# A norm applied behind the products of four projection units instead of ahead of them, and gate projections two blocks ahead in a grouped attention

## The chip, the cores and the metric

One core of a Trainium2 chip runs the whole program. The metric is the device time of one execution in microseconds (us). Four compute engines work side by side and meet at semaphores: PE (TensorE, matrix products into the eight banks of PSUM), DVE (VectorE), ACT (ScalarE) and POOL (GpSimd, which here never touches PSUM). SP starts most of the loads. Each engine runs its own list of instructions strictly in order.

## The reference, cut to what matters

The input (512 tokens of 1024 features, and 256 context tokens) goes through a first block (norm, two grouped attentions, gated up-projection, MLP) and then through two blocks with adaptive norms. The change touches two places. In the first block two gates are computed from the same normed input as the attention:

```python
y = jax.nn.sigmoid(gate_a) * (o_a @ w_up_nsa[l]) + jax.nn.sigmoid(gate_b) * (o_b @ w_up_swa[l])
...
f = jnp.square(jax.nn.relu(u @ w_mlp_in[l])) @ w_mlp_out[l]
h = h + rms_norm(f, norm_mlp_post[l])
```

and right behind that MLP the second block normalises the result and projects it to queries, keys, values and gates of eight heads:

```python
hx = modulate(rms_norm_2(x, norm_g[i]), shift_x[:, None], scale_x[:, None])   # h * (1 + scale) + shift
hc = modulate(rms_norm_2(ctx, norm_g[i]), shift_c, scale_c)
...
qx, kx, vx, gx = split(hx @ w_in)
qc, kc, vc, gc = split(hc @ w_in)
```

The norm's factor, one over the root mean square, is one number for each token; gain, scale and shift are one number for each feature. So hx @ w is that factor times ((x * gain * (1 + scale)) @ w), plus shift @ w.

## The kernel before, in words

Everything lies transposed, features on the 128 partitions and tokens along the row; a tensor of 1024 features is eight tiles k = 0 to 7 of 512 token columns (and 256 context columns). Weights come in **units** of 1024 x 128. Each unit is loaded by SP, rounded to fp32r on ACT (`split_high`, L330), and the rest of it is taken on POOL (`low`, L973). A product is then three matmuls for each k: high by high, low by high, high by low (`products`, L347 and L351). The units have one order through the whole program, and the slots of their two halves alternate between two places (`SPL`), with a few exceptions in the table `THIRD`. A unit's `split_high` waits until the unit before last is done on PE.

**The first grouped attention** (`A1`). After the phase "prep" all engines meet. PE does the scores of steps 0 and 1, then `attn_pe` walks 62 blocks of 128 keys: each block is a transposition of four heads' weights (L570), then a gate tile (`gate_tiles`, two k of a gate unit, six matmuls into bank 5), then the weighted sum of the block before (L581); scores of later steps (L551) stand between. DVE takes minima (L675) and scales (L710), ACT does the exponentials (L636) and moves the transposed block (L621). Every fourth block ACT moves a finished gate unit out (`gate_out`, L867), rounds the next unit, POOL multiplies the gate by the norm, and ACT later takes the tanh and stores it by DMA. The 16 gate units are 64 such tiles; the last two stand behind the last block, and then PE waits until the last output group is split on ACT (L745) and DVE (L750, semaphore `A1.ol`) and begins the up-projections.

**From the MLP to the first head.** The last MLP round ends with eight accumulations into `f_t`. PE sums their squares over the features (`column_sums`, L415, matmuls of one column each), ACT takes the root, DVE inverts, and `spread` (L430) brings the factor to all partitions in bank 5. DVE then scales and adds, tile by tile (L2087, L2093), giving `hc`; ACT squares each tile (L1578), PE sums each (`tile_sum`). In between PE does the context products of the first two units of the heads' projection, whose context input was made during the MLP. With the second root (L1580), DVE's reciprocal and a second `spread` into bank 7, the normed input is made: `x_tile` on DVE (L1988), `shift_tile` on ACT (L1527), `low_tile` on DVE (L1994), for k = 0 to 7, and units 0 and 1 follow them staggered; units 2 and 3 (value and gate) come whole through `project`. ACT evicts each (L1596 to L1602). DVE rotates queries and keys (`rotate`, L2123 to L2132, six operations each), and `gate_up` (L2138) makes the gate.

**The heads.** `attend` on PE does for each of eight heads the scores of six query tiles (L1311), transpositions of the weights (L1323) and the two weighted sums (L1347, L1355), and between them `dense(n)`, n of the 32 k-steps of the next head's four units (`project`). A k-step is six matmuls, three of 512 and three of 256 columns. On DVE `mins` (L2184) and `combine` (L2192 to L2199) work on each query tile, then the next head's two rotations; on ACT the exponentials (L1640), and `take` moves each finished unit out of the banks. `take` of the next head's key unit stands inside the fifth query tile's exponentials.

## Time and profile before

| what | value |
|---|---|
| median of 3 runs | 1629.29 us (1629.1 to 1634.57) |
| the profiled execution's own time | 1629.36 us |
| its span in the profile | 1627.2 us |
| mean granted clock of TensorE | 0.984 of full |
| PE busy | 1556.7 us, 96% |
| DVE, ACT, POOL busy | 985.8, 751.7, 504.6 us |
| share of PE in the chain that ended last | 80% |

The profile page gives busy times and, for the chain, which engine's work the end waited for at each step. The two places of the change lie at 130 to 335 us (the first attention) and at 788 to 899 us (from the last MLP product to the second head) of the span. The granted clock is given as a share of full speed: 1.00 is 2.4 GHz and 0.50 is 1.2 GHz.

### The profile page before, as it was taken

What the parts mean: (1) busy time and instruction counts of PE and PEld (TensorE: products, weight loads), DVE (VectorE), ACT (ScalarE), POOL (GpSimd) and SP (SyncE); (2) the same over time, 40 slices, a digit from 0 to 9 for tenths busy, and PEclk for the clock granted to TensorE, in tenths of its full rate; (3) what the DMA queues carried; (4) which work ended last, traced back from release to release, by engine and by line L of the source; (5) the groups of instructions that cost most, each with busy time, mean ns of one, the idle gap of its engine ahead of it and who ended that gap; (6) DMA issues with size and microseconds to landing.
All of it is one profiled execution on the core that took longest, in us unless ns stands there. A gap on an engine that the chain in (4) does not pass through costs nothing.

```text
span 1627.2 us, 23677 instructions
## 1 busy us (share of the span) xinstructions
PE 1556.7 (96%) x8392; PEld 1221.3 (75%) x8392; DVE 985.8 (61%) x2266; ACT 751.7 (46%) x1413; POOL 504.6 (31%) x231
## 2 busy tenths in 40 slices
PE   7998999999899999999899999999999989999997
PEld 5886666678688888888877877778777768876566
DVE  6235555355679867645666666675676267147854
ACT  6225766634342423234344554455445343248753
POOL 3651232245244444444221111121214354230012
PEclk9999999999999999999899999999999989999999
DMA  6861112264356565643111111111111122220001
GB/s 200 174 162 33 59 59 77 76 256 130 104 193 194 191 198 188 198 134 100 53 53 39 40 39 39 39 39 39 39 39 52 52 56 89 78 66 14 2 14 65
DMA packets 48401, 149.34 MB, mean 92 GB/s; under 512 B 5782, under 2 KB 9110, under 8 KB 48184
## 3 DMA queue, kind: packets, MB, share of 16 engines
q1 hardware_dynamic: 37080, 112.45, 23.0%
q10 hardware_dynamic: 11232, 35.72, 6.8%
q8 instruction: 54, 0.88, 0.2%
q14 instruction: 35, 0.29, 0.1%
HBM read 141.53 MB, written 6.62 MB: 91 GB/s over the span
## 4 chain that ended last, share of the span: by engine, by line
PE 80%; DVE 7%; ACT 5%; issue 5%; POOL 1%; DMA 1%; ACTq 0%; POOLq 0%; DVEq 0%; SPq 0%
PE ps L347 41%; PE ps L351 20%; PE ps L570 4%; PE ps L581 3%; PE ps L551 3%; PE ps L1347 3%; PE ps L1311 2%; PE ps L1323 1%; POOL w_l L973 1%; PE ps L415 1%; PE ps L1075 1%; ACT sb L636 1%; DVE tg L1921 1%; ACT w_h L330 1%; DVE b_sb L675 1%
## 5 line engine op out<-in xcount | busy, mean ns | idle before, releaser
L973 POOL TENSOR_TENSOR w_l<-raw,w_h 128x1024 fp32r<-128x1024 f32 (+1 forms) x190 | 457.0, 2406 | 897.1 <-ACT w_h L330 877.4
L330 ACT ACTIVATE w_h<-raw 128x1024 fp32r<-128x1024 f32 x190 | 200.7, 1058 | 360.5 <-PE ps L347 305.3
L347 PE MATMUL ps<-x2h,w_h 128*128 128x512 f32 (+1 forms) x816 | 245.3, 366 | 19.5 <-DVE x2l L1994 7.6
L347 PE MATMUL ps<-x1h,w_h 128*128 128x512 f32 x584 | 237.9, 407 | 16.0 <-POOL w_l L973 10.4
L347 PE MATMUL ps<-x2h,w_l 128*128 128x512 f32 (+1 forms) x816 | 231.8, 349 | 0.0
L351 PE MATMUL ps<-x2l,w_h 128*128 128x512 f32 (+1 forms) x816 | 231.7, 349 | 0.0
L347 PE MATMUL ps<-x1h,w_l 128*128 128x512 f32 x584 | 230.7, 395 | 0.0
L351 PE MATMUL ps<-x1l,w_h 128*128 128x512 f32 x584 | 230.1, 394 | 0.0
L347 PEld LDWEIGHTS ps<-x2h,w_h 128*128 128x128 f32 x816 | 132.4, 191 | 52.6 <-issue 17.1
L347 PEld LDWEIGHTS ps<-x2h,w_l 128*128 128x128 f32 x816 | 132.2, 191 | 20.8
L351 PEld LDWEIGHTS ps<-x2l,w_h 128*128 128x128 f32 x816 | 132.5, 191 | 19.5
L347 PEld LDWEIGHTS ps<-x1h,w_h 128*128 128x128 f32 x584 | 111.5, 191 | 40.5 <-POOL w_l L973 10.8
L347 PEld LDWEIGHTS ps<-x1h,w_l 128*128 128x128 f32 x584 | 111.1, 190 | 24.3
L351 PEld LDWEIGHTS ps<-x1l,w_h 128*128 128x128 f32 x584 | 111.7, 191 | 20.4
L2055 DVE CUSTOM_DVE_ANT_0 terms<-mraw,ps 128x1024 f32<-128x1024 f32 x96 | 116.8, 1216 | 2.5
L2184 DVE CUSTOM_DVE_ANT_0 a_p<-ps,small 128x768 f32<-128x768 f32 (+1 forms) x96 | 71.3, 776 | 58.4 <-issue 58.4
L347 PE MATMUL ps<-m_h,w_h 128*128 128x512 f32 x256 | 99.7, 389 | 0.0
L347 PE MATMUL ps<-m_h,w_l 128*128 128x512 f32 x256 | 99.6, 389 | 0.0
L351 PE MATMUL ps<-m_l,w_h 128*128 128x512 f32 x256 | 99.6, 389 | 0.0
L1640 ACT ACTIVATE a_p<-a_p,small 128x768 f32<-128x768 f32 (+1 forms) x96 | 75.2, 786 | 20.4 <-DVE small L2184 20.4
L980 POOL TENSOR_TENSOR g_stage<-g_stage,rstd 128x512 f32<-128x512 f32 x16 | 20.6, 1286 | 148.2 <-ACT g_stage L867 148.2
L636 ACT ACTIVATE sb<-sb,small 128x256 f32<-128x256 f32 (+4 forms) x128 | 59.7, 471 | 4.2 <-ACT g_stage L872 1.9
(318 smaller groups left out, 2615.3 us busy)
## 6 DMA issues: line engine op xcount, KB each, us to landing
raw<-in_w_mlp SPq DMA_DIRECT2D x64, 512.0 KB, 3.7
mraw<-in_w_mod ACTq DMA_DIRECT2D x51, 512.0 KB, 3.7
raw<-in_w_a SPq DMA_DIRECT2D x32, 512.0 KB, 3.6
raw<-in_w_att SPq DMA_DIRECT2D x25, 512.0 KB, 11.3
raw<-in_w_b SPq DMA_DIRECT2D x20, 512.0 KB, 3.6
raw<-in_w_g SPq DMA_DIRECT2D x16, 512.0 KB, 3.6
raw<-in_w_ao SPq DMA_DIRECT2D x9, 512.0 KB, 3.5
gates<-g_stage ACTq DMA_DIRECT2D x16, 256.0 KB, 2.2
```

The lines of the kernel that those rows point to most:

```text
L330: nc.scalar.activation(split(u)[0], raw[:, u % RAW], ACT.Copy).then_inc(w_hi, 1)
L347: mm = nc.tensor.matmul(o, w[:, k], xh(k), start=(first and k == k0 and wi == 0), stop=(last and k == k1 - 1 and wi == 1))
L351: mm = nc.tensor.matmul(o, w[:, k], xl(k), start=False, stop=False)
L551: mm = nc.tensor.matmul(A.sbank(m + h)[:, o:o + rhs.shape[-1]], st[qx](r + h), rhs, start=(x == 0), stop=(x == last), skip_group_check=True)
L570: mm = nc.tensor.transpose(ps[0:w, 4 + x % A.tb, y * P:(y + 1) * P], A.sb[n % A.sbn][:, r, o:o + w], ident[:])
L581: mm = nc.tensor.matmul(ps[h * HD:(h + 1) * HD, 6 + g % 2, cols], st["v"](h)[b], A.pt[0:w, x % 4, h * 2 * P:(h + 1) * 2 * P], start=(st["f ...
L636: nc.scalar.activation(buf, buf, ACT.Exp, bias=negm[:, c:c + 1], scale=-1.0, accum_out=sums[:, c:c + 1]).then_inc(A.e, 1)
L973: nc.gpsimd.tensor_tensor(l[:, ks], raw[:, u % RAW, ks], h[:, ks].bitcast(F32), ALU.subtract).then_inc(w_lo, 1)
L1347: mm = nc.tensor.matmul(ps[:, 6], a_v[:, b, :], a_pt[:, b, :], start=(b == 0), stop=(b == 5))
L1640: nc.scalar.activation(buf, buf, ACT.Exp, bias=negm[:, cc:cc + 1], scale=-1.0, accum_out=sums[:, cc:cc + 1]).then_inc(ha["e"], 1)
L2055: nc.vector.tensor_tensor_reduce(out=terms[:], in0=mraw[:, c % MRAW].rearrange("p k m -> p (k m)"), in1=cps[:, w, :], scale=0.5, scalar=0. ...
L2184: nc.vector.tensor_tensor_reduce(out=a_p[qt % 3][m][:, 0:n], in0=pair(1 + 2 * m)[:, 0:n], in1=zero.to_broadcast([P, n]), scale=1.0, scalar ...
```

## The change

The gate tiles run two blocks ahead: tiles 0 and 1 go between the scores of steps 0 and 1, block x does tile x + 2 and none is left behind the last block; ACT's `gate_out` is moved with them. Behind the MLP, the first four units of the heads' projection use an input without the norm's factor (`xph`, `xpl`), made tile by tile as `hc` is; the shift's part comes out of two more columns of the context product (258 instead of 256), and DVE multiplies each of the four results in PSUM by the factor, and ACT (or DVE, for the gate) adds the shift. The full input with the norm is made after that, for the other units. Nine of the 32 k-steps of head 1 stand ahead of head 0's first scores, and the gate of head 0 is finished between its two rotations. Unit 2 gets a place of its own (`w_h4`, `w_l4`).

```diff
-THIRD = {..., U_MLP + 2: 2}
+THIRD = {..., U_MLP + 2: 2, U_A + 2: 3}
+AHEAD = 2
...
-        A1.between_pe, A1.between_act = gate_tiles, gate_out
+        A1.between_pe, A1.between_act = lambda pe, x: gate_tiles(pe, x + AHEAD), lambda act, x: gate_out(act, x + AHEAD)
...
-            attn_scores(pe, A1, 0)
-            attn_scores(pe, A1, 1)
+            for x in range(AHEAD):
+                attn_scores(pe, A1, x)
+                gate_tiles(pe, x)
             attn_pe(pe, A1)
-            for x in range(A1.blk[-1], N_G * KT // 2):
+            for x in range(A1.blk[-1] + AHEAD, N_G * KT // 2):
                 gate_tiles(pe, x)
...
             nm3a.wait(pe, "add", KT - 1)
             column_sums(sqsum, 4, S, True, False)
+            pe.wait_ge(ml_f, 4 + N_MLP - 2)
+            first_ctx(0, 1, 0, 2)
             nm3a.wait(pe, "sq", KT)
             column_sums(sq[:, 1], 4, S, False, True).then_inc(nm3a.mm, 1)
+            first_ctx(0, 1, 2, 4)
             nm3a.wait(pe, "rc", 1)
             nm3c.wait(pe, "lo", KT)
             spread(5, 0, 4).then_inc(nm3a.r, 1)
+            first_ctx(0, 1, 4, KT)
             pe.wait_ge(ml_f, 4 + N_MLP)
-            first_ctx(0, 0, KT)
-            tile_sum(0)
-            first_ctx(1, 0, KT // 2)
-            tile_sum(1)
-            first_ctx(1, KT // 2, KT)
-            for k in range(2, KT):
+            first_ctx(1, 3, 0, KT)
+            for k in range(KT):
                 tile_sum(k)
+                nm3p.wait(pe, "lo", k + 1)
+                for j in range(2):
+                    mm = first_x(j, 2 * j, k, k + 1)
+                    if k == KT - 1:
+                        mm.then_inc(unit, 1)
+            first_x(2, 4, 0, 4)
             nm3b.wait(pe, "rc", 1)
             spread(7, 0, 4).then_inc(nm3b.r, 1)
-            for k in range(KT + LAG):
-                if k < KT:
-                    nm3b.wait(pe, "lo", k + 1)
-                    mm = first_x(0, k)
-                    ...
-                if k >= LAG:
-                    mm = first_x(1, k - LAG)
-            mm.then_inc(unit, 1)
+            first_x(2, 4, 4, KT)
+            nm3b.wait(pe, "src", KT)
+            first_ctx(2, 5, 0, KT).then_inc(unit, 1)
+            first_ctx(3, 6, 0, KT)
+            wait_head(pe, "k", (None, 0), 1, 1)
+            first_x(3, 2, 0, KT).then_inc(unit, 1)
...
+                lead = i is None and c == 0
+                if lead:
+                    dense(9)
+                    wait_head(pe, "g", head, 1, 1)
                 wait_head(pe, "ro", head, 2, 2)
                 scores(0)
-                dense(2 if more else 3)
+                dense(1 if lead else 2 if more else 3)
...
                 scores(1)
-                dense(4 if more else 3)
+                dense(2 if lead else 4 if more else 3)
                 for qt in range(4):
                     scores(qt + 2)
-                    dense(2 if more else 4 + (qt == 0))
+                    dense(1 if lead else 2 if more else 4 + (qt == 0))
                     turns(qt)
-                    dense(1 + qt % 2 if more else 3)
+                    dense(1 + qt // 2 if lead else 1 + qt % 2 if more else 3)
                 turns(4)
-                dense(4)
+                dense(2 if lead else 4)
...
-            project((None, 0), 2 * KT, 2 * KT)
             pe.wait_ge(ha["ones"], 1)
             all_heads(pe, attend)
```

On ACT:

```diff
             mlp(3, False, True)
+            split_high(act, U_A + 2)
...
             for k in range(KT):
                 nm3b.wait(act, "src", k + 1)
+                nc.scalar.activation(xph[:, k, :], hc[:, k, 0:S], ACT.Copy, scale=mulx[:, 0, 0, k:k + 1]).then_inc(nm3p.hi, 1)
...
+            nm3b.wait(act, "r", 1)
+            nc.scalar.activation(rstd[:, 0:S], ps[:, 7], ACT.Copy).then_inc(n3_r, 1)
+            split_high(act, U_A + 3)
+            def take_first(j, dst, scale):
+                wait_head(act, "em", (None, 0), 8, 2 * j + 2)
+                nc.scalar.activation(dst[:, S:SC], ps[:, 2 * j + 1, 0:C], ACT.Copy, scale=scale)
+                return nc.scalar.activation(dst[:, 0:S], ps[:, 2 * j], ACT.Identity, bias=shifted[:, j:j + 1], scale=scale)
+            take_first(0, a_q, -0.125).then_inc(ha["q"], 1)
+            take_first(1, a_k, 1.0).then_inc(ha["k"], 1)
             for k in range(KT):
                 nm3b.wait(act, "t", k + 1)
-                shift_tile(k, 0, xn3, 0).then_inc(nm3b.hi, 1)
+                shift_tile(k, 0, xn2, 0).then_inc(nm3b.hi, 1)
+                if k == 3:
+                    split_high(act, U_A + 4)
             nc.scalar.activation(dev[:, 6:7], eps_t, ACT.Tanh)
+            take_first(2, a_vT, 1.0).then_inc(ha["v"], 1)
+            wait_head(act, "em", (None, 0), 8, 8)
+            nc.scalar.activation(a_g[0][:, S:SC], ps[:, 6, 0:C], ACT.Tanh, scale=0.5)
+            nc.scalar.activation(a_g[0][:, 0:S], ps[:, 2], ACT.Tanh, scale=0.5).then_inc(ha["gt"], 1)
+            split_high(act, U_A + 5)
...
+                if lead:
+                    wait_head(act, "ro", head, 2, 1)
+                    take((None, 1), 0, True)
```

On DVE:

```diff
-            for k in range(KT + 1):
-                ...
+            g_scale(0)
+            g_add(0)
+            g_scale(1)
+            for k in range(KT):
+                if 1 <= k < KT - 1:
+                    g_scale(k + 1)
+                    g_add(k + 1)
+                g_low(k)
+                if k == 0:
+                    g_add(1)
...
+            def evict_first(j, bank, ctx_bank, scale):
+                unit_done(v, U_A + j)
+                nc.vector.tensor_scalar(shifted[:, j:j + 1], ps[:, ctx_bank, C:C + 1], scale, None, ALU.mult).then_inc(ha["em"], 1)
+                nc.vector.tensor_tensor(ps[:, bank], ps[:, bank], rstd[:, 0:S], ALU.mult).then_inc(ha["em"], 1)
             invert(v, nm3b, S)
-            modulated(nm3b, 0, xn3, (0,))
+            v.wait_ge(n3_r, 1)
+            evict_first(0, 0, 1, -0.125)
+            evict_first(1, 2, 3, 1.0)
+            modulated(nm3b, 0, xn2, (0,))
+            evict_first(2, 4, 5, 1.0)
+            unit_done(v, U_A + 3)
+            done(nc.vector.tensor_copy(shifted[:, 3:4], ps[:, 6, C:C + 1]))
+            nc.vector.tensor_tensor(ps[:, 2], ps[:, 2], rstd[:, 0:S], ALU.mult).then_inc(ha["em"], 1)
+            settle(v)
+            wait_head(v, "em", (None, 0), 8, 7)
+            nc.vector.tensor_scalar(ps[:, 2], ps[:, 2], shifted[:, 3:4], None, ALU.add).then_inc(ha["em"], 1)
...
             rotate((None, 0), 0, "q")
+            wait_head(v, "gt", (None, 0), 1, 1)
+            done(nc.vector.scalar_tensor_tensor(out=a_g[0][:, S:SC], ..., in1=ps[:, 6, 0:C], ...))
+            nc.vector.scalar_tensor_tensor(out=a_g[0][:, 0:S], ..., in1=ps[:, 2], ...).then_inc(ha["g"], 1)
+            settle(v)
             rotate((None, 0), 1, "k")
             nc.vector.tensor_copy(ones_r[:], ones[:]).then_inc(ha["ones"], 1)
-            gate_up((None, 0))
```

## Rows read from the trace of the kernel before

**Rows 1.** Page, part 4: shares of the chain that ended last, by engine.

```profile
PE 80%; DVE 7%; ACT 5%; issue 5%; POOL 1%; DMA 1%; ACTq 0%; POOLq 0%; DVEq 0%; SPq 0%
```

**Rows 2.** Windows of 1 us; third number from the right is the granted clock.

```profile
131.00:132.00 1.00, 0.50 (x8) 0.30 (x6) 0.55 (x5) 0.14 (x1) 1.00 (x1) 0.98 0.00 0
...
295.00:296.00 1.00, 0.37 (x2) 0.37 (x3) 1.00 (x10) 1.00 (x5) 0.00 (x0) 0.90 0.81 328
...
790.00:791.00 1.00, 0.49 (x5) 0.40 (x4) 0.16 (x1) 0.45 (x2) 0.60 (x1) 0.87 0.00 0
...
797.00:798.00 1.00, 1.00 (x8) 1.00 (x7) 1.00 (x3) 0.39 (x1) 0.00 (x0) 0.72 0.00 0
...
807.00:808.00 1.00, 1.00 (x10) 1.00 (x10) 0.00 (x0) 0.05 (x1) 0.00 (x0) 0.90 0.00 0
```

**Rows 3.** Timeline, PE, MLP to second head: start, us, engine, line.

```profile
791.35 2.07 PE L430 MATMUL ps<-ident,small 128*128 128x128 f32 x8 [0.87 <-DVE small L425]
...
802.53 0.28 PE L347 MATMUL ps<-x2h,w_l 128*128 128x256 f32 x1
...
802.65 5.71 PE L415 MATMUL ps<-ones,sq 128*128 128x1 f32 x48
...
828.78 0.39 PE L347 MATMUL ps<-x2h,w_l 128*128 128x512 f32 x1
...
829.00 0.51 PE L347 MATMUL ps<-x2h,w_h 128*128 128x512 f32 x2
...
846.05 0.50 PE L1311 MATMUL ps<-a_kh,a_qh 64*128 64x512 f32 x2
...
848.10 0.59 PE L347 MATMUL ps<-x2h,w_h 128*128 128x512 f32 x2 [0.73 <-DVE a_g L2138]
...
899.32 0.50 PE L1311 MATMUL ps<-a_kh,a_qh 64*128 64x512 f32 x2
```

**Rows 4.** Timeline, DVE, the same pattern of scale, add and low earlier in the program.

```profile
433.30 0.69 DVE L1960 TENSOR_TENSOR hc<-hc,f_t 128x512 f32<-128x512 f32 x1
...
443.53 0.69 DVE L1960 TENSOR_TENSOR hc<-hc,f_t 128x512 f32<-128x512 f32 x1
```

**Rows 5.** Timeline, DVE, first and last of the eight normed tiles.

```profile
811.04 1.40 DVE L1988 SCALAR_TENSOR_TENSOR xn<-hc,small,ps 128x512 f32<-128x512 f32 x2 [2.17 <-PE ps L430]
...
821.25 1.62 DVE L1994 SCALAR_TENSOR_TENSOR x2l<-xn,small,x2h 128x512 fp32r<-128x512 f32 x2
```

**Rows 6.** Timeline, DVE beside POOL, and an undisturbed rotation.

```profile
826.38 2.22 DVE L2123 TENSOR_TENSOR ropea<-a_q,cos_t 128x512 f32<-128x512 f32 x1 [3.50 <-ACT a_q L1596]
...
1362.98 1.43 DVE L1994 SCALAR_TENSOR_TENSOR x2l<-xn,small,x2h 128x256 fp32r<-128x256 f32 x2
...
1361.33 2.40 POOL L973 TENSOR_TENSOR w_l<-raw,w_h 128x1024 fp32r<-128x1024 f32 x1 [3.03 <-ACT w_h L330]
...
879.70 0.68 DVE L2123 TENSOR_TENSOR ropea<-a_q,cos_t 128x512 f32<-128x512 f32 x1
...
884.18 0.69 DVE L2123 TENSOR_TENSOR ropea<-a_k,cos_t 128x512 f32<-128x512 f32 x1
```

**Rows 7.** Timeline, ACT: table load, high half, two-part move.

```profile
822.11 1.28 ACT L1585 ACT_TABLE_LOAD   x1
...
824.52 1.06 ACT L330 ACTIVATE w_h<-raw 128x1024 fp32r<-128x1024 f32 x1 [0.91 <-PE ps L347]
...
1229.30 1.04 ACT L1619 ACTIVATE ao_t<-ps,small 128x512 f32<-128x512 f32 x2
```

**Rows 8.** Timeline, the first attention's end, PE and DVE.

```profile
331.02 1.08 PE L581 MATMUL ps<-pt,v_all 128*64 128x256 f32 x8
...
334.90 0.39 PE L347 MATMUL ps<-o1h,w_h 128*128 128x512 f32 x1
...
332.78 0.69 DVE L750 TENSOR_TENSOR o1l<-ps,o1h 128x512 fp32r<-128x512 f32 x1 [3.73 <-ACT o1h L745]
```

**Rows 9.** Timeline, PE, the second block's transposition in the first attention.

```profile
140.13 0.66 PE L570 MATMUL ps<-ident,sb 128*128 128x128 f32 x4
```

More of the change, by code:

```diff
@@ L307, in split @@
                 return w_h3[:], w_l3[:]
+            if THIRD.get(u) == 3:
+                return w_h4[:], w_l4[:]
             if u >= N_ATT:
@@ L327, in split_high @@
                     act.wait_ge(up_free, 4)
+            elif i is None and u == U_A + 2:
+                act.wait_ge(unit, U_A)
             else:
@@ L445, in build @@
         n3_sum = sem("n3_sum")
+        n3_r = sem("n3_r")
         fin_g = sem("fin_g")
@@ L995, in _ @@
                     low(U_MLP + j, i, 16)
-            lows(U_A, U_AO + 1)
+            for u in range(U_A, U_A + 4):
+                low(u)
+            lows(U_A + 4, U_AO + 1)
             g.wait_ge(ha["lo"], KT - 2)
@@ L1177, in _, with first_ctx, first_x, tile_sum @@
             mlp(3, range(8, 16))
+            def first_ctx(j, bank, k0, k1):
+                split_ready(pe, U_A + j)
+                return products(U_A + j, [(ps[:, bank, 0:C + 2], lambda k: x2h[:, k, S:SC + 2], lambda k: x2l[:, k, S:SC + 2])],
+                                k0, k1, first=(k0 == 0), last=(k1 == KT),
+                                ready=(lambda k: nm3c.wait(pe, "lo", k + 1)) if j == 0 else None)
+            def first_x(j, bank, k0, k1):
+                split_ready(pe, U_A + j)
+                return products(U_A + j, [(ps[:, bank], lambda k: xph[:, k, :], lambda k: xpl[:, k, :])], k0, k1,
+                                first=(k0 == 0), last=(k1 == KT))
+            def tile_sum(k):
+                nm3b.wait(pe, "sq", k + 1)
+                column_sums(sq[:, k % 2], 6, S, k == 0, k == KT - 1).then_inc(n3_sum, 1)
             nm3a.wait(pe, "add", KT - 1)
             column_sums(sqsum, 4, S, True, False)
+            pe.wait_ge(ml_f, 4 + N_MLP - 2)
+            first_ctx(0, 1, 0, 2)
             nm3a.wait(pe, "sq", KT)
             column_sums(sq[:, 1], 4, S, False, True).then_inc(nm3a.mm, 1)
+            first_ctx(0, 1, 2, 4)
             nm3a.wait(pe, "rc", 1)
@@ L1483, in _ @@
             attn_act(act, A1)
-            for x in range(A1.blk[-1], 4 * N_G + 2):
+            for x in range(A1.blk[-1] + AHEAD, 4 * N_G + 2):
                 gate_out(act, x)
@@ L1602, in take @@
                     nc.scalar.activation(a_g[c % 2][:], src, ACT.Tanh, scale=0.5).then_inc(ha["gt"], 1)
-                if ahead and (j == 3 or not begins):
+                if ahead:
                     split_high(act, U_A + 4 * c + j + 2, i, 8)
@@ L1663, in attend @@
                 exps(1, 1)
-                if more:
+                if more and not lead:
                     take((i, c + 1), 0, True)
-                else:
+                elif not more:
                     take_out(0)
@@ L1688, in attend @@
                     take_out(6)
-            for j in range(4):
-                take((None, 0), j, True)
             all_heads(act, attend)
```

90 lines of the change are left out of this document (48 added, 42 removed).

## The prediction

> **What bounds the kernel now.** I read the chain of waits first: PE carries 80% of it [rows 1], so time is won only where PE stands still or runs slowly, and where its work is taken away. The change takes no product away. So I looked at the two places for holes, with windows of 1 us and PE's timeline. In the first attention TensorE's granted clock falls to 1.2 GHz in the window from 131, after PE had waited at the meeting of the engines, and once more from 295 behind short waits [rows 2]. Behind the MLP it falls twice: in the window from 790, during sums of one column and short waits, back at 797; and in the window from 807, where PE was busy all the time, but with 5.71 us of such sums [rows 2, 3]. These and the wait for the normed tiles are what could be won: head 0's scores start at 846.05 and head 1's at 899.32 [rows 3]. I follow the change up to the latter; behind it the heads are the same.
>
> **Part 1, gate tiles two blocks ahead.** A tile of two k costs 1.43 us: the four k left at the end fill the 2.87 from 332.03 (331.02 + 1.01, the next start) to 334.90 [rows 8]. Moved to the start, two tiles stand where PE waited for DVE. There the second block's transposition began at 140.13 [rows 9], with a tile in front of it at half rate. With the tiles PE fills most of the holes; if the clock then stays up, I count 130.8 + 0.7 (scores) + 1.4 (tile) + 0.7 (scores) + 1.4 (tile) + 0.6 (scores), then a wait for DVE's first scaling until 135.9 (0.5 later than before, since its minima start later), + 0.4 + 1.4 + 0.6 + 0.7 = 138.9: 1.2 won. If it falls as before, the tiles cost double and 1.5 are lost. At the end the cover goes: PE waits for the last output's two halves, about 1.97 after the last product (ACT 0.6 in, 0.4 later than now since a gate's move and a unit's high half are queued ahead of it, then DVE's 0.69 [rows 8]) instead of 2.87 of tiles: 0.9 won. What the new wait may do is drop the clock, as near 295: some 3.3 us at half rate cost 1.65, so 0.75 lost. ACT's moves, POOL's factor and the gates' stores keep their distance to their tile; the last gate's store and SP's loads behind it come about 3 us earlier and hide. Sum: start -1.2, end between -0.9 and +0.75, taken as -0.1: **-1.3**, bounds -2.1 and +2.3.
>
> **Part 2, step by step.** Costs from rows 3: a context matmul 0.12 (802.53 to 802.65), a 512-column one 0.22 to 0.23 (828.78 to 829.00), a column sum 5.71/6 = 0.95, a k-step of both 1.066 (16 from 829.00 to 846.05), a spread 2.07 at half rate, so about 1.1 at full.
> Up to the first spread: ACT now rounds unit 2 (1.06 [rows 7]) ahead of the root, which moves the spread from 791.35 to 791.8. The context products put into the waits are free. Then 12 k of context, 36 x 0.12 = 4.3. At full clock PE is through at 791.8 + 1.1 + 4.3 = 797.2; if the clock falls as before and returns at 797.4, at 799.9.
> The loop: per k one sum and six matmuls, 0.95 + 1.35, and 0.08 for the first weights behind a sum, 2.38. DVE's scale, add and low take (443.53 - 433.30)/5 = 2.05 per k [rows 4], ACT's two passes less, so PE bounds: 19.0. POOL's low half of unit 2 ends near 795 and holds DVE's first add for 1.6, still in time. Half of unit 2 (12 x 0.225 = 2.7) and the spread follow. I call the end of the spread E: 820.0 at full clock, 822.8 if it had fallen. I take the middle, **821.4**.
> From E the path is DVE's. PE has 2.7 + 2.9 + 2.9 + 5.4 for units 2 and 3 and 8 x 1.066 for unit 4: done at E + 22.5, then it wants the next query (ACT's `take` behind `rotate`) for its ninth step, and both rotations for the scores. DVE and ACT: factor moved by ACT 0.65; two evictions on DVE, 0.17 + 0.65 each with starts, to E + 2.4; ACT rounds unit 3 (to E + 1.6) and moves queries and keys, 1.05 each [rows 7], to E + 3.8; only then its shifts. The eight normed tiles take 822.87 - 811.04 = 11.8 [rows 5], start late by 0.6, and are held by unit 4 inside them: ACT's 1.06, and POOL's low half, which holds a DVE operation with two SBUF inputs until it ends: 1362.98 + 1.43 is 0.68 behind POOL's end of 1363.73 [rows 6]. Before, POOL was idle here. Together +1.8: E + 16.6. Two evictions and a shift on DVE 2.4: E + 19.0. Beside it ACT loads a table (1.28 [rows 7]), moves the values, then takes the gate's tanh, 1.1, to E + 20.2, and rounds unit 5, so POOL runs from E + 21.2 to 23.6. A rotation takes 4.48 (879.70 to 884.18), but an operation beside POOL waits it out (2.22 instead of 0.68) [rows 6]: queries at E + 25.9 instead of 23.5. The gate 1.2, then the keys, again held, since the next unit's high half follows the next `take`: **E + 33.1**. So PE idles from E + 22.5 to 26.8 and from 27.8 to 33.1, and scores start at 854.5 instead of 846.05.
> Head 0: before 899.32 - 846.05 = 53.3. Nine k-steps less, 9.6; the wait of 0.73 for the gate gone [rows 3]. Added: unit 5 is now finished two query tiles earlier against the scores, and the first k of unit 6 needs the keys moved out, which ACT does inside the fifth tile's exponentials: DVE's combine and minima and ACT come 2.3 after PE. And after 9 us nearly idle the clock is surely down; behind the spread of 791.35 it took some 4 to 5 us of products, until 797, to return [rows 2, 3], so 2.0 lost. 53.3 - 9.6 - 0.7 + 2.3 + 2.0 = 47.3, and head 1 starts at 854.5 + 47.3 = 901.8: **+2.5**.
> Bounds: the clock's first fall, E from 820.0 to 822.8 (1.4 either way); the rotations and low halves undisturbed by POOL, down to E + 28 (5 less); the wait for the keys 0 to 4; the clock in the head 0 to 4.6.
> The rest: two more columns a product add 0.02 us; the shift's columns are a few values on DVE in the MLP's last round, and DVE is busy for only 985.8 us of the whole; the higher stride of x2 moves nothing. SP's loads keep their order; unit 4 to 6 load as soon as their low half is taken, long before. Nothing is left out.
>
> **The sum.** -1.3 + 2.5 = +1.2 on the profiled execution's 1629.36: **1630.6**. That execution lies 0.07 above the median, so the same number stands for it.
>
> **A rule against part of it.** The clock fell at 807 with PE busy in every part of the window [rows 2]. The Trainium skill ("TensorE: Matmul & The Clock Gate", Part 1) calls the lower rate the state of an idle array and says that activity releases it. By that rule PE, now given products in its waits behind the MLP, keeps 2.4 GHz, E is 820.0, and the sum would be 1629.2; by the row of 807, sums count for little and the fall comes as before, 1632.0.
>
> **The rivals.** (a) Sign other than mine: the normed path leaves PE's way. If DVE had both rotations when PE has its ninth step, head 0's scores start at E + 23.5 = 844.9, no clock is lost, and head 1 starts at 844.9 + 45.3 = 890.2, 9.1 earlier: with part 1 the run takes 1619.0. For it: the count of DVE's path is long, and each held operation is a guess on order. Against it: even undisturbed it is E + 28. I give it, with half of it or more, 0.2. (b) Slower: head 0's clock stays down. With 23 k-steps instead of 32 among waits for DVE, PE is less dense; if 1.2 GHz holds over the first 20 us of the head, 10 us are lost instead of 2, from the moment that the clock does not return within about 10 us of the first scores: 1638.6, 0.07. For it: the fall at 807 with a busy PE; against it: the falls in rows 2 ended once products of 512 columns ran, and those still make half of the head. (c) The fall behind the MLP is gone and nothing else differs, the rule's case: 1629.2, 0.2. (d) Part 1 loses at both ends, +2.3: 1634.2, 0.1. My own case has the rest, 0.43.
>
> **How the numbers follow.** About 0.5%, 8.1 us, is what a measurement of this kernel can tell from no change. Of (a) most of the way is needed for that: 0.15 faster. Of the slower ones only (b) and a sum of bad bounds: 0.06. Same 0.79. My case alone runs from 1626 to 1635; the range reaches down towards (a) and up to (d) with a bad head: 1621.0 to 1636.5.
>
> **What would show it.** After: no half-rate windows in the first attention's start, and PE waiting about 2 us on DVE's L750 row at its end; the loop of sums and products taking 19 us; DVE's normed tiles beside a POOL low half and longer than 11.8; PE waiting twice between unit 4 and the first scores, near 844 to 855; a wait for the keys' move in head 0 of about 2. Wrong if PE has no wait of over 2 us there, or if head 1's scores start before 895 or after 906 (with part 1's shift taken off).

## The result, and the profile after

The changed kernel takes **1641.82 us** (median of 5 runs, 1639.61 to 1644.70); the kernel before took 1629.29. The ratio is 1.0067, with a 95% interval of 1.0050 to 1.0085: about 11 us slower by the ratio. The prediction was 1630.6 with a range up to 1636.5, so it was wrong, and on the side that I had given 0.06.

The profiled execution of the kernel after took 1641.82 us, with a span of 1639.9 (before: 1629.36 and 1627.2). Line numbers are those of each kernel's own profile: the products stand at L358 and L362 now, and at L347 and L351 before.

The shares of the chain that ended last, the page's part 4 [rows 1]:

```profile
PE 76%; DVE 8%; ACT 6%; issue 4%; DMA 4%; POOL 2%; ACTq 0%; POOLq 0%; SPq 0%; DVEq 0%
```

PE's share fell from 80% to 76%. So I asked next what PE waited for over the whole span, in the table of waits (us in total, times, longest):

```profile
PE ps L358 <- DVE ones_r L2319: 15.7, 1, 15.7
PE ps L358 <- POOL w_l L986: 10.8, 3, 10.2
PE ps L358 <- DVE x1l L2009: 5.1, 5, 3.5
...
```

One wait of 15.7 us, for a tile that my prediction does not name: `ones_r`, the ones in rounded form, which the head's sum of squares multiplies by (first at 909.7 here). Before, there was no such wait. PE's timeline round it [rows 3] (start, us, engine, line):

```profile
792.78 2.07 PE L441 MATMUL ps<-ident,small 128*128 128x128 f32 x8 [0.16 <-DVE small L436]
...
820.34 1.05 PE L441 MATMUL ps<-ident,small 128*128 128x128 f32 x8
...
834.93 0.39 PE L358 MATMUL ps<-xph,w_l 128*128 128x512 f32 x1
850.99 1.01 PE L358 MATMUL ps<-x2h,w_h 128*128 128x512 f32 x2 [15.67 <-DVE ones_r L2319]
...
863.44 0.59 PE L358 MATMUL ps<-x2h,w_h 128*128 128x512 f32 x2 [1.05 <-ACT a_q L1638]
...
864.66 0.50 PE L1332 MATMUL ps<-a_kh,a_qh 64*128 64x512 f32 x2
...
882.83 0.58 PE L358 MATMUL ps<-x2h,w_h 128*128 128x512 f32 x2 [2.32 <-ACT a_k L1640]
...
910.50 0.50 PE L1332 MATMUL ps<-a_kh,a_qh 64*128 64x512 f32 x2
```

Unit 3's last product ends at 835.3, and unit 4's first starts at 850.99. Nothing that unit 4 multiplies is missing by then, as DVE's timeline shows:

```profile
823.40 1.40 DVE L2032 SCALAR_TENSOR_TENSOR xn<-hc,small,ps 128x512 f32<-128x512 f32 x2
...
831.11 2.11 DVE L2038 SCALAR_TENSOR_TENSOR x2l<-xn,small,x2h 128x512 fp32r<-128x512 f32 x1
...
835.37 1.62 DVE L2038 SCALAR_TENSOR_TENSOR x2l<-xn,small,x2h 128x512 fp32r<-128x512 f32 x2
...
841.18 2.82 DVE L2213 TENSOR_TENSOR a_q<-ropea 128x512 f32<-128x512 f32 x1
...
849.84 0.96 DVE L2217 TENSOR_TENSOR a_kl<-a_k,a_kh 128x768 fp32r<-128x768 f32 x1
850.72 0.22 DVE L2319 CAST ones_r<-ones 128x128 fp32r<-128x128 f32 x1
```

The last normed tiles were done at 836.99. But DVE copies the ones behind both rotations, and PE has `pe.wait_ge(ha["ones"], 1)` on its queue ahead of all heads. Before, that wait stood behind `project((None, 0), 2 * KT, 2 * KT)`, the 16 steps of units 2 and 3 [rows 3: 829.00 to 846.05], and the copy was done under them. The change took the `project` away and put unit 4's steps into head 0, behind the wait. The line stands in the change's own diff, unmarked, and I had read past it.

The clock followed (windows of 1 us; third number from the right is the granted clock):

```profile
839.00:840.00 1.00, 0.00 (x0) 0.00 (x0) 1.00 (x4) 0.78 (x3) 0.00 (x0) 0.95 0.00 0
840.00:841.00 1.00, 0.00 (x0) 0.00 (x0) 0.96 (x2) 1.00 (x2) 0.00 (x0) 0.50 0.00 0
...
856.00:857.00 1.00, 1.00 (x5) 0.84 (x4) 0.00 (x0) 0.00 (x0) 0.00 (x0) 0.52 0.06 16
857.00:858.00 1.00, 1.00 (x7) 0.86 (x7) 0.00 (x0) 0.00 (x0) 0.00 (x0) 1.00 0.00 0
```

It is at 1.2 GHz from 839.9 to 856.5, so the first three of unit 4's steps take 1.9 us each instead of 1.05. Of that fall, PE stands idle for the first 11 us; from 850.99 to 856.5 it works at half rate, which by the windows costs about 2.7 us.

**Where the 12.7 us of the span lie.** The MLP's last product starts at 788.61 instead of 787.47: 1.1, of which 0.6 are there before the first attention begins. From it to head 1's scores it takes 121.9 instead of 111.85: **10.0**. From there to the end, where nothing was changed, 729.4 instead of 727.9: 1.5. The last kind is noise between executions. In the fourteen profiled executions of this study that stretch took 727.9 to 731.9 us. Much of that spread goes with how long the clock was down in the norm behind the heads. I count each window of 1 us between 1299 and 1339 as 1 less its granted clock: the four executions with 5.1 us there took 728.2 to 729.4, the four with 8.5 took 731.0 to 731.9, and the six with 6.8 lie anywhere from 727.9 to 730.9. For a mechanism I therefore read one stretch of the trace, above all MLP's last product to head 1, and leave the rest to the medians.

### The profile page after: what moved, and what is told of

Same layout as the page of the kernel before. It is cut to its first block, busy times and chain, and to the rows that moved or that the text cites. A ratio compares the mean times of both kernels' runs of the same rounds, so it can differ in the third digit from the quotient of the medians.

```text
span 1639.9 us, 23714 instructions
## 1 busy us (share of the span) xinstructions
PE 1555.2 (95%) x8392; PEld 1219.9 (74%) x8392; DVE 995.0 (61%) x2286; ACT 758.3 (46%) x1426; POOL 504.0 (31%) x231
## 4 chain that ended last, share of the span: by engine, by line
PE 76%; DVE 8%; ACT 6%; issue 4%; DMA 4%; POOL 2%; ACTq 0%; POOLq 0%; SPq 0%; DVEq 0%
PE ps L358 39%; PE ps L362 19%; PE ps L583 3%; PE ps L594 3%; DMA raw<-in_w_att 3%; PE ps L564 3%; PE ps L1332 3%; PE ps L1372 3%; POOL w_l L986 1%; PE ps L1344 1%; ACT w_h L341 1%; DVE tg L1965 1%; PE ps L426 1%; DVE x2l L2038 1%; DVE b_sb L688 1%
## 5 line engine op out<-in xcount | busy, mean ns | idle before, releaser
L358 PE MATMUL ps<-x2h,w_h 128*128 128x512 f32 (+2 forms) x784 | 234.6, 364 | 34.2 <-DVE ones_r L2319 15.7
L358 PE MATMUL ps<-x1h,w_h 128*128 128x512 f32 x584 | 236.6, 405 | 17.7 <-POOL w_l L986 10.8
L358 PE MATMUL ps<-x1h,w_l 128*128 128x512 f32 x584 | 229.4, 393 | 0.0
L362 PE MATMUL ps<-x1l,w_h 128*128 128x512 f32 x584 | 228.9, 392 | 0.0
L362 PE MATMUL ps<-x2l,w_h 128*128 128x512 f32 (+2 forms) x784 | 221.4, 347 | 0.0
L358 PE MATMUL ps<-x2h,w_l 128*128 128x512 f32 (+2 forms) x784 | 221.2, 347 | 0.0
L358 PEld LDWEIGHTS ps<-x2h,w_h 128*128 128x128 f32 x784 | 127.3, 191 | 63.4 <-issue 19.0
L358 PEld LDWEIGHTS ps<-x1h,w_h 128*128 128x128 f32 x584 | 110.7, 190 | 42.8 <-POOL w_l L986 11.4
L358 PEld LDWEIGHTS ps<-x2h,w_l 128*128 128x128 f32 x784 | 127.2, 190 | 19.6
L362 PEld LDWEIGHTS ps<-x2l,w_h 128*128 128x128 f32 x784 | 127.4, 191 | 19.0
L358 PEld LDWEIGHTS ps<-x1h,w_l 128*128 128x128 f32 x584 | 110.4, 189 | 24.0
L362 PEld LDWEIGHTS ps<-x1l,w_h 128*128 128x128 f32 x584 | 110.8, 190 | 20.2
L358 PE MATMUL ps<-m_h,w_h 128*128 128x512 f32 x256 | 99.7, 389 | 0.0
L358 PE MATMUL ps<-m_h,w_l 128*128 128x512 f32 x256 | 99.6, 389 | 0.0
L362 PE MATMUL ps<-m_l,w_h 128*128 128x512 f32 x256 | 99.6, 389 | 0.0
```

What stands on the lines that cost most here:

```text
L358: mm = nc.tensor.matmul(o, w[:, k], xh(k), start=(first and k == k0 and wi == 0), stop=(last and k == k1 - 1 and wi == 1))
L362: mm = nc.tensor.matmul(o, w[:, k], xl(k), start=False, stop=False)
```

## The experiments

**1. The copy of the ones moved.** In the changed kernel:

```diff
             invert(v, nm3b, S)
+            nc.vector.tensor_copy(ones_r[:], ones[:]).then_inc(ha["ones"], 1)
             v.wait_ge(n3_r, 1)
...
             rotate((None, 0), 1, "k")
-            nc.vector.tensor_copy(ones_r[:], ones[:]).then_inc(ha["ones"], 1)
```

> The changed kernel with one instruction moved: the copy of the ones (0.22 us on DVE), which stood behind both rotations, now stands where DVE waits for ACT's move of the factor. Theory A, TensorE's wait for that copy ahead of all heads is what I overlooked: the eight k of unit 4 start at once at about 835.2 (they took 8 x 1.05 at full clock) and end at 843.7, PE then waits for the queries' move (rotation at 845.5, 1.05 for ACT, so about 846.6), does the ninth step, waits until 850.8 for the keys' rotation, and head 0's scores start at 851 to 852 instead of 864.66. Head 1 starts 10 to 13 us earlier than in the changed kernel, and the run takes 1629 to 1632. Rival B, the copy is only the last of several things that come late together (the rotations, the low tiles beside POOL, the clock), and the wait moves on to the rotations: under 4 us won, 1638 or more. Rival C, the clock at 1.2 GHz behind the idle time costs most: the wait goes but head 0 stays slow, 1633 to 1637.

Measured: 1631.20 (11 runs) beside 1631.10 for the kernel before on the same chip, ratio 1.0000 (0.9990 to 1.0009). The whole loss is gone. PE's and DVE's timelines:

```profile
847.50 0.58 PE L358 MATMUL ps<-x2h,w_h 128*128 128x512 f32 x2 [2.95 <-ACT a_q L1638]
853.74 0.80 PE L1332 MATMUL ps<-a_kh,a_qh 64*128 64x512 f32 x2 [4.43 <-DVE a_kl L2218]
```

```profile
848.73 2.55 DVE L2212 TENSOR_TENSOR ropea<-ropea,sin_t 128x512 f32<-128x512 f32 x1
```

Now PE waits where I had put its waits: for the queries' move, then for the keys' rotation, with an operation of that rotation held beside POOL. The second spread ends at 822.25 here, so the scores start 31.5 behind it. The stretch from the MLP's last product to head 1 is 109.3, against 121.9 and, before, 111.85; 1.15 of the 12.6 is a fall of the clock right behind the MLP that did not come here. A's numbers hold; B and C are out. The stretch is 2.5 shorter than before although the medians are equal; experiment 4 finds 1.6 lost by part 1, in the first attention and right behind it.

**2. The wait put into the kernel before**, so that the mechanism is seen with nothing else of the change:

```diff
-            project((None, 0), 2 * KT, 2 * KT)
             pe.wait_ge(ha["ones"], 1)
+            project((None, 0), 2 * KT, 2 * KT)
```

> The kernel before with nothing but the order of two lines on TensorE's queue turned round: the wait for the copy of the ones now stands ahead of the products of units 2 and 3, as it stands ahead of unit 4 in the changed kernel. The copy ends at 839.0, the products start at 829.0. Theory A: PE idles for 10 us, the clock falls, the first three steps run at half rate (2.5 us), and the run takes 11 to 13 us longer than before, 1642 to 1644. Rival B, other work makes the delay and the wait is harmless: within 2 us of before.

Measured: 1641.99 beside 1630.35, ratio 1.0073 (1.0057 to 1.0088).

```profile
828.52 0.39 PE L347 MATMUL ps<-x2h,w_l 128*128 128x512 f32 x1
838.72 1.01 PE L347 MATMUL ps<-x2h,w_h 128*128 128x512 f32 x2 [9.81 <-DVE ones_r L2228]
```

Head 0 starts at 857.15 instead of 846.05, 11.1 later, and it is never made up: head 1's scores come 123.2 behind the MLP's last product instead of 111.85. Two lines in the other order cost as much as the whole change did.

**3. The clock's part.** In the changed kernel PE gets 60 products into a bank whose next product starts anew, ahead of the wait:

```diff
+            for n in range(60):
+                nc.tensor.matmul(ps[:, 0], xph[:, 0, 0:P], xph[:, n % KT, :], start=(n == 0), stop=(n == 59))
             pe.wait_ge(ha["ones"], 1)
```

> The changed kernel with 60 products of 512 columns (13.5 us at 0.225 each) into an unused bank where PE stands in the wait for the ones, so that the wait stays and only the clock is kept up. If the clock's fall to 1.2 GHz (839 to 856.5) is a part of the loss, it is the 2.5 to 2.8 us by which the first steps of unit 4 were slow: 1639 where the changed kernel took 1641.8, with scores at 862. If the clock made the most of the loss, it would come down to 1632 or so; if the clock falls in spite of the products, nothing changes.

Measured: 1644.15 beside 1630.35, ratio 1.0081 (1.0066 to 1.0096), which cannot be told from the changed kernel's 1.0067. In the trace the products keep 2.4 GHz, and then the 2.2 us that are left of the wait are enough for a fall:

```profile
850.84 0.62 PE L358 MATMUL ps<-x2h,w_h 128*128 128x512 f32 x2 [2.18 <-DVE ones_r L2321]
```

```profile
852.00:853.00 1.00, 1.00 (x5) 0.81 (x4) 0.00 (x0) 0.00 (x0) 0.00 (x0) 0.50 0.00 0
```

Head 0's scores come 73.8 behind the MLP's last product instead of 76.05, 2.3 less. But half of this lies ahead of the wait: the second spread ends 31.6 behind the MLP's last product here and 32.8 in the changed kernel, whose clock fell once more right behind the MLP. From the end of the spread to the scores it is 42.2 instead of 43.3, so the filler gave back 1.1, not the 2.5 expected: the long fall (2.7 us of work at half rate lost) went, and a shorter one behind the remaining 2.18 us of wait came. So of the 10.0 us that the stretch had lost, the rows put 2.7 on the slow clock and leave some 7 to idle time; no run had the wait without any fall. The stretch behind head 1 took 731.9 here, 2.5 more than in the changed kernel, and the medians show no gain.

**4. The two parts apart.** Part 1 alone in the kernel before (only the three edits with `AHEAD`), and the changed kernel with `AHEAD = 0` and the first two blocks' scores as before:

> The kernel before with part 1 alone: the gate tiles two blocks ahead. By the marks of the profiled run of the changed kernel (up projection starts at 334.31 where it was 334.90, while the start of the first attention was 0.6 later for reasons outside of the change) it wins 0.5 to 1.3 us: 1628 to 1629. Rival: the +1.0 to +1.2 us that stand at the up and out projections' later marks (381.16 against 379.98 for the first product of the output projection) come from the missing tiles, so part 1 costs about 1 us: 1630.5.

> The changed kernel with part 1 undone (gate tiles at their old places), so the deferred norm alone. Theory A: the whole loss is behind the MLP, so it takes as long as the changed kernel or up to 1.3 us longer, 1641 to 1643.5, and head 0's scores start about 18 us later than before. Rival: part 1 carries several us of the loss, 1638 or less.

Measured: part 1 alone 1632.02, ratio 1.0004 (0.9995 to 1.0013); the norm alone 1638.62, ratio 1.0044 (1.0030 to 1.0058), both beside 1631.10. So the norm carries the loss, if with 7.5 rather than 11 or 12. Its stretch of the trace, MLP's last product to head 1, is 119.6, with the same wait of 15.67; of the 2.3 by which it is shorter than the changed kernel's, 1.1 is a fall of the clock behind the MLP that did not come, and 1.2 a shorter fall behind the wait. Part 1 alone does nothing that the medians can tell. Its two ends can be read in the changed kernel [rows 8, 9], PE and then DVE:

```profile
139.78 0.66 PE L583 MATMUL ps<-ident,sb 128*128 128x128 f32 x4
...
331.39 1.08 PE L594 MATMUL ps<-pt,v_all 128*64 128x256 f32 x8
334.31 0.50 PE L358 MATMUL ps<-o1h,w_h 128*128 128x512 f32 x1 [1.83 <-DVE o1l L763]
```

```profile
333.56 0.69 DVE L763 TENSOR_TENSOR o1l<-ps,o1h 128x512 fp32r<-128x512 f32 x1 [5.43 <-ACT o1h L758]
```

At the start no window is at half rate any more, and the second block's transposition comes 0.35 earlier, 1.0 with the 0.64 taken off by which the first scores came late. That holds in all six executions with two tiles ahead, although in two of them (experiment 3 and the first try of experiment 6) a fall of 1.7 comes at 147 or 148 instead. At the end, from the start of the last output's products to the up projection's first product, it is 2.92 instead of 3.88 (331.02 to 334.90), 0.96 won. Then the clock falls from 334.9 to 338.4: from the up projection's first product to the output projection's it takes 46.85 us instead of 45.08. PE waits 1.83 there in every execution with two tiles ahead, and in five of six the clock fell behind it (the changed kernel, experiments 1 and 3, part 1 alone, and experiment 7); in none of the executions without part 1 did it fall there.

The prediction had nothing between the two ends, and there is a loss. From the second block's transposition to the last output's products, part 1 alone takes 192.7 where the kernel before takes 190.9, each with one fall near 295; without that fall the changed kernel takes 191.6, and experiment 5, which has no tiles ahead, 189.3. So about 2 us are lost on the way. One of them can be seen in the changed kernel: POOL's factor for a gate now falls on DVE's scaling of the attention weights, four operations that took 1.14 in experiment 5 (320.45), and PE waits for it, DVE, POOL and PE:

```profile
320.37 2.18 DVE L723 TENSOR_SCALAR sb<-sb,small 128x256 f32<-128x256 f32 x4
321.13 1.27 POOL L993 TENSOR_TENSOR g_stage<-g_stage,rstd 128x512 f32<-128x512 f32 x1 [7.92 <-ACT g_stage L880]
322.60 0.66 PE L583 MATMUL ps<-ident,sb 128*128 128x128 f32 x4 [1.61 <-DVE sb L723]
```

The wait at the same block is 0.57 in experiment 5. I have not traced the rest of the loss. Up to the output projection, part 1 alone then needs 250.8 us from the first scores where the kernel before needs 249.2: 1.6 lost, beside a median that is 0.9 higher and not clear of noise.

**5. The norm with the ones early, without part 1.**

> The deferred norm alone with the copy of the ones early (part 1 undone). If part 1 costs what its runs show (the clock's fall at 336 behind the new wait, 1.75 us between the first products of the up and the output projection, against about 1 won at the start), this one is 0.5 to 1.5 us faster than the version with both, so 1629.5 to 1631 where the kernel before has 1631. If part 1 is worth nothing either way: within 0.4 us of it, 1631.

Measured: 1629.81 beside 1630.35, ratio 0.9995 (0.9986 to 1.0005). The deferred norm, freed of the wait, gains nothing that can be measured, and lies within the interval of experiment 1, so the run cannot tell the two expectations apart. The stretch from the MLP's last product to head 1 is 110.8, 1.0 shorter than before.

**6. What stands in its way.** In experiment 1 PE still waits 2.95 and 4.43 ahead of the scores. First try: unit 5's high half right behind the last normed tile, and twelve steps instead of nine ahead of the scores, three fewer in head 0:

```diff
                 if k == 3:
                     split_high(act, U_A + 4)
+                if k == 7:
+                    split_high(act, U_A + 5)
...
-                    dense(9)
+                    dense(12)
```

> The changed kernel with the copy of the ones moved as in the first experiment, unit 5's high half taken on ACT right behind the last normed tile, so that POOL's low half falls on evictions from PSUM and not on the queries' rotation, and twelve k-steps instead of nine ahead of the scores (three fewer in head 0's first two blocks). Theory A: DVE ends the keys' rotation at about 848.7 instead of 850.8 (the operation of 2.82 us at 841.18 goes back to 0.69), PE waits once, about 843.7 to 844.5, and is busy until the scores; head 1 starts 3 to 5 us earlier than in the first experiment: 1625 to 1628. Rival: head 0 is bound by DVE's chain of minima and combinations once its products are fewer, and what is won ahead of the scores comes back as waits in the head: the same as the first experiment within 1 us.

Measured: 1631.34 (0.9994, 0.9985 to 1.0004). The rival was right. The rotation of the queries is all but undisturbed (its first operation takes 1.09 instead of 0.68, where 2.86 had been held in experiment 1), but the hold on the keys' stayed (2.58 at 845.90). Inside head 0 PE waited 1.11 and 1.95 for DVE's minima, where the products were now missing, and 2.30 for the keys' move, as it had before. The stretch is 108.3, one better than experiment 1.

Second try, on top of it: unit 6's high half only once both rotations are done, the next head's keys moved out by ACT behind query tile 0 instead of inside tile 4, the steps spread as 12, 1, 1 and then singly, and part 1 left out:

```diff
                 if lead:
                     wait_head(act, "ro", head, 2, 1)
-                    take((None, 1), 0, True)
+                    take((None, 1), 0, False)
+                    wait_head(act, "ro", head, 2, 2)
+                    split_high(act, U_A + 6)
...
-                        if qt == 2 and more:
+                        if qt == 2 and more and not lead:
                             take((i, c + 1), 1, True)
...
                     turned(qt)
+                    if qt == 0 and lead:
+                        take((i, c + 1), 1, True)
```

> The version that should beat both kernels. Over the one with twelve steps ahead it has: the gate tiles at their old places (part 1 undone), unit 6's high half taken only behind the keys' rotation, so that POOL's low half no longer holds one of the rotation's operations (2.58 us at 845.90 there), the next head's keys moved out by ACT two query tiles earlier, and the products spread as 12, 1, 1 and then one at a time. Theory A: head 0's scores start about 2 us earlier against the end of the MLP (61.4 us behind the MLP's last product there, 59.5 here), PE's waits of 1.11, 1.95 and 2.30 inside head 0 are gone or under 1 in all, and head 1 starts 103 to 105 us behind the MLP's last product instead of 108.3: 1625 to 1627 in the median, 4 to 6 below the kernel before. Rival: DVE's chain of minima and combinations bounds head 0 once PE has one k-step at a time beside it, the waits only change places, and head 1 stands at 107 or more: 1629 to 1630.

Measured: **1623.26** beside 1630.35, ratio 0.9949 (0.9935 to 0.9962). PE's waits from 780 to 915:

```profile
PE ps L358 <- ACT a_q L1638: 1.5, 2, 1.2
PE ps L358 <- ACT a_k L1640: 0.8, 1, 0.8
PE ps L1331 <- DVE small L2274: 0.7, 1, 0.7
...
```

The stretch is 100.5 us where the kernel before needs 111.85; PE's wait for the rotations is gone altogether. Of the 7.9 by which it is shorter than in the first try, 1.9 lie ahead of head 0's scores, which now come 27.9 behind the second spread instead of 29.8, and the rest in head 0 (41.0 instead of 46.9). The first is unit 6's, as experiment 7 shows; in head 0 the keys' earlier move and the new spread of the steps were changed together, and no run tells them apart.

**7. The last pieces, on one chip.** The rescheduled version again; the same with one gate tile ahead; with two; and without tiles ahead, but with unit 6's high half back in its old place. The tiles' edit, with `AHEAD` 1 or 2:

```diff
+            for x in range(2):
+                attn_scores(pe, A1, x)
+                if x < AHEAD:
+                    gate_tiles(pe, x)
```

> The rescheduled version with the gate tiles at their old places, once more, beside the three that follow: 1623 to 1625, 6 to 8 below the kernel before.

> The rescheduled version with the gate tiles one block ahead instead of none. If the start's gain comes with the first tile and the end's loss only when nothing is left under the last output (1.43 us of products left against a wait of about 1.97), it has both: no fall of the clock at 132 to 139, no fall behind 334 or a wait of 0.5 that is too short for one: 0.5 to 1 us below the version without. Rival: the start needs both tiles (the fall comes after the second block's scores), and then it equals the version without within 0.4.

> The rescheduled version with part 1 as in the changed kernel. By the marks of the runs so far it loses 1.75 us between the first products of the up and the output projection (the fall at 336) and wins about 1 at the start, so it is 0.5 to 1 us above the version without, and no better than 0.3 below it if both cancel.

> The rescheduled version with one thing taken back: unit 6's high half again right behind the queries' move, so that POOL's low half runs beside the keys' rotation. DVE's rotation operation takes 2.6 us instead of 0.69, the scores of head 0 start 1.9 us later, and as PE has nothing else there, head 1 and the end come 1.5 to 1.9 later too: 1625 to 1626. Rival: head 0 is bound elsewhere and swallows it: within 0.5 us of the version without.

Measured, beside 1632.33 for the kernel before:

| version | median, us | ratio, 95% interval | MLP's last product to head 1 |
|---|---|---|---|
| no tile ahead | 1619.24 | 0.9926 (0.9910 to 0.9942) | 101.6 |
| one tile ahead | **1618.43** | 0.9916 (0.9901 to 0.9931) | 100.6 |
| two tiles ahead | 1621.85 | 0.9936 (0.9922 to 0.9951) | 100.5 |
| none, unit 6 not late | 1623.73 | 0.9944 (0.9929 to 0.9959) | 102.4 |

The first came out 4 us below what I expected from its run before. One tile ahead is the fastest seen, but its interval and that of no tile overlap, so only its place ahead of the kernel before is sure. Two tiles come out 2.6 over none, where 0.5 to 1 was expected, but these intervals overlap as well. Between one tile and two the executions hardly meet (1615.6 to 1620.0 against 1619.9 to 1622.8). The profile of one tile shows what was hoped for. The first attention has no window at half rate, and PE goes on without a wait from the last output into the up projection:

```profile
330.40 0.40 PE L358 MATMUL ps<-x1h,w_l 128*128 128x512 f32 x1
330.64 0.50 PE L358 MATMUL ps<-o1h,w_h 128*128 128x512 f32 x1
```

With two tiles ahead the same place has the wait and the fall behind it:

```profile
333.37 0.65 PE L358 MATMUL ps<-o1h,w_h 128*128 128x512 f32 x1 [1.83 <-DVE o1l L763]
```

The rival for one tile, that the start needs both, was wrong. The first attention in three parts, in us, shows that one tile has the gain at both ends and not the loss between:

| version | first scores to second transposition | to the last output's products | to the up projection | fall near 295 |
|---|---|---|---|---|
| kernel before | 9.35 | 190.9 | 3.88 | yes |
| part 1 alone | 8.37 | 192.7 | 2.91 | yes |
| no tile (experiment 5) | 10.37 | 189.3 | 3.88 | no |
| one tile | 8.37 | 189.2 | 2.51 | no |
| two tiles | 8.37 | 191.6 | 2.91 | no |

With one tile the four scaling operations take 1.14 again (317.74), with two 2.18. Each row is one execution, and the fall near 295 comes in some executions and not in others of the same code (experiment 1 has it, the changed kernel has not), so only rows with the same entry there are to be compared.

With unit 6 not late the hold is back, and PE waits for it:

```profile
845.29 2.59 DVE L2214 TENSOR_TENSOR ropea<-ropea,sin_t 128x512 f32<-128x512 f32 x1
```

```profile
850.33 0.50 PE L1331 MATMUL ps<-a_kh,a_qh 64*128 64x512 f32 x2 [1.87 <-DVE a_kl L2220]
```

That wait of 1.87 is the 1.9 expected, and no fall of the clock followed it. Counted from the end of the second spread, head 0's scores come 29.8 and without the hold 27.9 behind it, and head 0 takes 41.0 in both. (The stretches of the table differ by only 0.8, since the clock fell behind the MLP in the profiled execution without the hold and not in this one.) The medians differ by 4.5, more than the mechanism explains. The same version took 1623.26 on the chip of experiment 6, so differences of 2 to 4 us between versions that ran apart are not to be read as an effect.

## Why the prediction was wrong, point by point

**The step that failed** is the one sentence "done at E + 22.5, then it wants the next query (ACT's `take` behind `rotate`) for its ninth step". I followed unit 4's data (the tiles, the weights) and not PE's queue. Between unit 3 and unit 4 stood a wait that I had read over, because in the kernel before it costs nothing and no row of its trace shows it. With E at 821.39 unit 4 ended not at E + 22.5 but at 862.4, E + 41. The prediction's two waits, near 844 to 855, were one of 15.67 and one of 1.05, and head 1's scores, at 910.50, were past the 906 that it had named as a sign of being wrong. Experiments 1 and 2 show this from both sides: without the wait the change costs nothing, and with it alone the old kernel loses 11.6 us in the median. The question for a removed step is what its work hides and what that costs without the cover. I asked it for the eight tiles and the evictions, but not for the `project` of units 2 and 3, which hid the copy. "Nothing is left out" was said of the small terms, and the largest was missing.

**Part 1**, predicted -1.3 (start -1.2, end -0.1, bounds -2.1 and +2.3). The start was right: 1.0 won, no fall (in two of the six executions one came 15 us later). The end was at its bad bound: PE waited 1.83 (I had 1.97), 0.96 was won against my 0.9, and the clock fell, which cost 1.77 where I had 1.65. I took the middle between fall and no fall, but it fell in five executions of six. The step that failed here is "keep their distance to their tile", which put everything between the ends at nothing: it kept the distance to the tile but not to DVE's scaling, and about 2 us went there. Part 1 alone stands at +1.6 at the output projection, not at -1.3, inside the bounds only by its bad end.

**E.** I had 821.4 with the MLP ending at 787.47, 33.9 behind its last product; measured 32.8. The fall at 807 is gone, although PE does the same eight one-column sums, now with products between them; the fall at 791 came in this execution (792 to 796) and cost about 1.1: in the nine executions of the deferred norm without it the spread ends 31.6 behind the MLP. **The rule of the Trainium skill** that I weighed ("TensorE: Matmul & The Clock Gate", Part 1: the lower rate is the default, and activity releases it) was nearer than my row of 807. In the eleven executions of the deferred norm, where PE has products in its waits, the clock fell at 807 in none and behind the MLP's last product in two; in the three of the old order it fell at both places in each. The rule does not fit the kernel before at 807, where the array was busy by the profile's count and the clock fell. What PE did differs, six sums in a row there and one sum for every six products here; no run changes only that.

The prediction's words that the falls "ended once products of 512 columns ran" do not fit the fall of 790, which ended at 797 under context products of 256 columns. The loop's pitch was 2.26 (804.77 less 802.51 for the first product behind a sum) where I had 2.38.

**DVE's path from E.** The tiles took 13.6 (I had 11.8 + 1.8 = 13.6), the queries' rotation had one operation held (2.82), and the whole path ended at E + 29.4, not E + 33.1: the second hold did not come, since ACT's next `take` was itself late. In experiment 1, where it was not, the hold came and the keys were ready at E + 31.4, my figure within 1.7. The Trainium skill ("SBUF — State Buffer", the section "SBUF: two separate sides") says that an operation of VectorE with two SBUF inputs and one of GpSimd that reads SBUF exclude each other, and that the later one waits to the end. The trace agrees: 2.82, 2.55, 2.58 and 2.59 us for operations that take 0.69 alone, and the moved evictions, which read PSUM, kept their 0.69 beside POOL's low half of unit 5 in experiment 6. But two inputs are not needed for a hold in this case. In the kernel before, the rounding of the queries at 830.74, an operation with one SBUF input, takes 2.63 beside POOL's low half where it takes 0.56 alone, and the scaling of experiment 4 has one such input beside a factor for each partition.

**Head 0** took 45.8 (I had 47.3), with the wait of 2.32 for the keys' move (I had 2.3).

**The rivals.** (a), the normed path off PE's way, did not come by itself; it took the rescheduling of experiment 6, and then head 1's scores stood at 885.3 to 891.3, where (a) had 890.2. (b) was about a low clock in head 0: the clock was low for 17 us ahead of it, but in 11 of them PE stood idle, and inside head 0 it fell once, for 3.4 us at 884, behind the wait for the keys. Of (c) the fall at 807 went, and E came 1.1 earlier against the MLP. Of (d) only the end came; the start was won, and the loss between the ends was in no case. So 1.1 won and 1.6 lost nearly cancelled, by luck and not as forecast. The real case was none of the four, and it had no chance of its own.

## What to carry to other kernels

When a change takes work away or moves it, go down the engine's queue line by line from where it stood and ask of every wait behind it, however old, what that work covered; a wait that costs nothing has no row in the profile. A wait that guards one late instruction (here one sum of squares 60 us on) belongs beside that instruction, or its producer belongs early. And the loss seen in a wait's row may hide that the freed schedule is still unbalanced: the deferred norm was worth nothing until ACT's and POOL's halves and the keys' move were put elsewhere, and then 7.1 us in one set of runs and 13.1 in another. Moving PE's work by two blocks also moves what the other engines do for it: with two tiles ahead POOL's factor came to lie on DVE's scaling, with one it did not.

## What the runs showed of the hardware that I had not expected

A wait of 2.18 us was enough for the clock to fall after 13 us of dense products (experiment 3), and one of 1.83 at the first attention's end did it in five executions of six. But behind 1.87 ahead of head 0's scores the clock stayed up for 6 us and more in both executions that had it (the first try of experiment 6, and unit 6 not late), 2.32 for the keys' move did it in the changed kernel and not in experiment 1, and 1.2 ahead of the ninth step did it in none of the six executions of experiments 6 and 7. So the length of the wait alone does not tell whether the clock falls. The commonest single fall lost 1.7 us of clock.

Summed up to 1600 us (windows of 1 us, each 1 less its granted clock, idle time included) the losses were 12.0 us with one tile ahead, 23.9 in the kernel before, 22.2 in the changed one and 27.3 with the wait put into the kernel before. In the norm behind the heads the same instructions lost 5.1 in one execution and 8.5 in another, so two executions of one kernel differ by whole falls.
